# Attention of a diffusion block on TensorE: one query tile of both heads per step, scores two steps ahead, and half of the modulation slabs loaded into the place of the split weights

## The reference, cut to what matters

```
mod  = silu(c) @ w_mod[layer] + b_mod[layer]        # 6 vectors of 1024, for latents and for context
h    = modulate(rms_norm(x, norm1_g), sh1, sc1)
px   = h @ w_in[layer]                              # q, k, v of branches A and B, u of C, gates
y_a  = softmax(q_a k_a' / 8) v_a                    # 8 heads, 512 keys for latents, 256 for context
y_b  = softmax(q_b k_b' / 8 + bias) v_b             # 4 heads, the bias on latent keys only
y_c  = pool_mixer(u)
m    = sum of sigmoid(gate) * (y @ w_branch)        # then w_out and a gated residual
x    = x + g2 * ffn(modulate(rms_norm(x), sh2, sc2))    # dense in layer 0, 8 experts in layer 1
```

## Time and profile before

| | us |
|---|---|
| median of 3 runs (2268.6 to 2272.04) | 2270.48 |
| the profiled execution | 2268.39 |
| its span, first to last instruction | 2266.5 |
| TensorE busy | 2140.1 (94%) |
| attention of layer 0, first scores to the end of the last transpose | 142.55 to 258.85 |
| attention of layer 1, the same | 991.01 to 1072.20 |

### The profile page before, as it was taken

One profiled execution on the slowest core, in us unless ns is written; L12 is line 12 of the kernel. 1 busy time (PEld: TensorE's weight loads), 2 busy tenths in 40 slices (PEclk: granted clock), 3 DMA queues, 4 the chain that ended last, 5 costly groups with the idle time before them and its releaser, 6 DMA issues.

```text
span 2266.5 us, 27521 instructions
## 1 busy us (share of the span) xinstructions
PE 2140.1 (94%) x10750; PEld 1589.7 (70%) x10751; DVE 1147.7 (51%) x1353; ACT 1051.7 (46%) x1139; POOL 1272.5 (56%) x466
## 2 busy tenths in 40 slices
PE   5988899998999998887998999999999999999997
PEld 3874577647788787864997777776767777776775
DVE  2146311231010103345324887878778787878776
ACT  4223322014212123323324766766666666766665
POOL 2300233114545443400421989988988989988996
PEclk8999999998999999898997999999999999999999
DMA  7325521222222222225445999989999999989993
GB/s 296 111 94 223 207 93 75 75 74 103 102 80 106 77 91 93 92 104 205 162 162 204 371 337 353 358 334 352 346 341 345 347 340 351 357 333 352 346 346 142
DMA packets 69640, 503.16 MB, mean 222 GB/s; under 512 B 7744, under 2 KB 7872, under 8 KB 9088
## 3 DMA queue, kind: packets, MB, share of 16 engines
q1 hardware_dynamic: 68976, 497.92, 58.8%
q0 software_dynamic: 528, 3.41, 0.4%
HBM read 500.24 MB, written 1.05 MB: 221 GB/s over the span
## 4 chain that ended last, share of the span: by engine, by line
PE 49%; POOL 32%; issue 12%; DVE 3%; DMA 2%; ACT 1%; SPq 0%; POOLq 0%; DVEq 0%; ACTq 0%
POOL moe_lo L482 31%; PE bank L756 12%; PE bank L758 11%; PE bank L757 11%; PE bank L771 7%; PE bank L784 2%; PE turned L955 2%; PE pv_bank L974 1%; DMA start_slab<-in_w_mod 1%; PE bank L934 1%; DVE s_mx L1859 1%; DMA slab<-in_w_in 1%; POOL w_lo L446 1%; ACT H_NEW L1359 0%; PE bank L939 0%
## 5 line engine op out<-in xcount | busy, mean ns | idle before, releaser
L482 POOL TENSOR_TENSOR moe_lo<-moe_slab,moe_hi 128x512 fp32r<-128x512 f32 x336 | 916.0, 2750 | 163.1 <-ACT moe_hi L1543 161.8
L482 DVE TENSOR_TENSOR moe_lo<-moe_slab,moe_hi 128x1536 fp32r<-128x1536 f32 x336 | 688.3, 2053 | 175.0 <-ACT moe_hi L1543 172.6
L446 POOL TENSOR_TENSOR w_lo<-slab,w_hi 128x2048 fp32r<-128x2048 f32 (+3 forms) x72 | 293.1, 4072 | 741.8 <-ACT w_hi L1316 741.7
L1543 ACT ACTIVATE moe_hi<-moe_slab 128x2048 fp32r<-128x2048 f32 x336 | 629.5, 1906 | 0.1
L756 PE MATMUL bank<-moe_hi,HE_HI 128*96 128x512 f32 x896 | 360.3, 402 | 1.3 <-POOL moe_lo L482 1.2
L758 PE MATMUL bank<-moe_hi,HE_LO 128*96 128x512 f32 x896 | 353.1, 394 | 0.0
L757 PE MATMUL bank<-moe_lo,HE_HI 128*96 128x512 f32 x896 | 351.7, 392 | 0.0
L756 PE MATMUL bank<-H_HI,w_hi 128*128 128x512 f32 (+1 forms) x880 | 325.6, 370 | 17.9 <-POOL H_LO L660 12.7
L757 PE MATMUL bank<-H_LO,w_hi 128*128 128x512 f32 (+1 forms) x880 | 321.9, 366 | 0.0
L758 PE MATMUL bank<-H_HI,w_lo 128*128 128x512 f32 (+1 forms) x880 | 321.8, 366 | 0.0
L1316 ACT ACTIVATE w_hi<-slab 128x2048 fp32r<-128x2048 f32 (+1 forms) x72 | 135.6, 1883 | 166.6 <-PE bank L758 147.8
(11 more groups left out here) (199 smaller groups left out, 2481.9 us busy)
## 6 DMA issues: line engine op xcount, KB each, us to landing
moe_slab<-in_moe_up SPq DMA_DIRECT2D x224, 1024.0 KB, 4.8
moe_slab<-in_moe_w SPq DMA_DIRECT2D x112, 1024.0 KB, 4.8
slab<-in_w_mod SPq DMA_DIRECT2D x40, 1024.0 KB, 4.8
slab<-in_w_in SPq DMA_DIRECT2D x38, 1024.0 KB, 4.8
slab<-in_ffn_w SPq DMA_DIRECT2D x30, 1024.0 KB, 4.8
start_slab<-in_w_mod SPq DMA_DIRECT2D x8, 1024.0 KB, 18.0
slab<-in_w_proj SPq DMA_DIRECT2D x8, 1024.0 KB, 6.9
slab<-in_w_out SPq DMA_DIRECT2D x8, 1024.0 KB, 4.9
```

What stands on the lines that cost most here:

```text
L446: engine.tensor_tensor(lo, raw, hi.bitcast(F32), ALU.subtract).then_inc(done, 1)
L482: engine.tensor_tensor(moe_lo[n][:, blocks, :], moe_slab[k % MOE_RING][:, blocks, :], moe_hi[n][:, blocks, :].bitcast(F32), ALU.subtract). ...
L1543: af(moe_hi[k % MOE_SPLIT][:], moe_slab[k % MOE_RING][:], ACT.Copy).then_inc(moe_hi_ready, 1)
```

## The change

A step is now one query tile of both heads of a latent pair, or both query tiles of both heads of a context pair: 18 steps in layer 0, 12 in layer 1. Scores are made two steps ahead. In each step TensorE makes the scores of step n + 2, one piece of modulation, the transposes of step n, and, where the step before ended a pair, the values of that pair. Bank `turned[g]` holds head g, and ScalarE copies both banks; VectorE copies none. The table is replaced by a rule: of three steps, two have a `mod` and the third a `turned_mod`. The `mod` of every step with n % 3 == 1 (`OUT_OF_RING`) no longer goes through the ring: its two slabs are loaded to `side_slab`, four buffers that lie where `w_hi` and `w_lo` lie. SyncE loads them between the ring's loads, the first two pairs when the last split matmul of the projection (`u`, 1) is done, the others when the `mod` two before in the same place is done. Before the first `high_part` after the attention ScalarE waits for these `mod`s.

The core of the diff:

```diff
+def attention_steps(layer):
+    return [(p, t) for p, (_, _, stream) in enumerate(attention_pairs(layer))
+            for t in range(2 if stream == LAT else 1)]
-MOD_IN_ATTENTION = (
-    [((p + 2) // 2 if p and p % 2 == 0 else None, None, 4 + p) for p in range(12)],
-    [(None, None, 16), (None, 17, 18), (8, None, 19), (9, 20, 21), (10, None, 22), (None, None, 23)])
+MOD_FIRST = (4, 16)
+def mod_beside(layer, s):
+    return None if s % 3 == 2 else MOD_FIRST[layer] + 2 * (s // 3) + s % 3
+def turned_beside(layer, s):
+    return MOD_FIRST[layer] // 2 + s // 3 if s % 3 == 2 else None
...
+        side_slab = [at(f"side_slab{i}", 24 + 8 * i, [P, DC, 256]) for i in range(4)]
...
+            def side_load(i):
+                n = OUT_OF_RING.index(i)
+                layer = int(i >= MOD_FIRST[1])
+                if i < MOD_FIRST[layer] + 4:
+                    wait_full(sp, ("in", layer, ("u", 1)))
+                else:
+                    wait_full(sp, ("mod", OUT_OF_RING[n - 2]))
+                for m in range(2):
+                    sp.dma_start(side_slab[2 * (n % 2) + m][:].rearrange("p k n -> p (k n)"), a["w_mod"][2 * i + m])\
+                        .then_inc(side_in[n % 2], 16)
...
+                if order[n][0] == "mod" and order[n][1] % 2 == 0:
+                    i = order[n][1] // 2
+                    first = MOD_FIRST[i >= MOD_FIRST[1]]
+                    if i == first + 2:
+                        side_load(i - 1)
+                        side_load(i + 1)
+                    elif i > first + 2 and i + 1 in OUT_OF_RING:
+                        side_load(i + 1)
...
 # TensorE
+                def turn(n):
+                    stream = pairs[steps[n][0]][2]
+                    for g in range(2):
+                        pe.wait_ge(p_ready[layer], 2 * n + g + 1)
+                        if n:
+                            pe.wait_ge(turned_out[layer], 2 * n + g - 1)
+                        for t in range(4):
+                            if stream == LAT:
+                                src = P * t
+                            else:
+                                kt, qt = divmod(t, 2)
+                                src = S * qt + P * kt
+                            ins = nc.tensor.transpose(turned[g][:, P * t:P * t + P], PR[:, n % 2, g, src:src + P], ident)
+                        ins.then_inc(turned_full[layer], 1)
...
+                scores(0)
+                scores(1)
+                for n in range(len(steps)):
+                    if n + 2 < len(steps):
+                        scores(n + 2)
+                    if mod_beside(layer, n) is not None:
+                        mod(mod_beside(layer, n))
+                    else:
+                        turned_mod(turned_beside(layer, n))
+                    turn(n)
+                    if n and last_step(layer, n - 1) is not None:
+                        values(last_step(layer, n - 1), n - 1)
+                values(len(pairs) - 1, len(steps) - 1)
...
 # ScalarE
                 exps(0)
+                for n in range(len(steps)):
+                    if n + 1 < len(steps):
+                        exps(n + 1)
+                    if ended(n - 2) is not None:
+                        result(ended(n - 2))
+                    turned_copy(n)
+                if ended(len(steps) - 2) is not None:
+                    result(ended(len(steps) - 2))
+                for i in OUT_OF_RING:
+                    if (i >= MOD_FIRST[1]) == layer:
+                        wait_full(act, ("mod", i))
                 for _ in range(2):
                     high_part()
                 result(len(pairs) - 1)
...
 # VectorE
                 maxima(0)
                 maxima(1)
+                for n in range(len(steps)):
+                    normalise(n)
+                    if n + 2 < len(steps):
+                        maxima(n + 2)
+                    if mod_beside(layer, n) is not None:
+                        mod(mod_beside(layer, n))
+                    else:
+                        turned_mod(turned_beside(layer, n))
```

More of the change, by code:

```diff
@@ L117, in mod @@
     def mod(i):
-        if i not in MOD_AT_START:
+        if i not in MOD_AT_START and i not in OUT_OF_RING:
             slabs.extend([("mod", 2 * i), ("mod", 2 * i + 1)])
@@ L150, in schedule, with scores @@
         fills.extend(("in", layer, ("u", m)) for m in range(layer, 2))
[L151 to L168, removed]
+        steps = len(attention_steps(layer))
+        def scores(n):
+            if n < steps:
+                fills.extend(("score", layer, n, g) for g in range(2))
+        scores(0)
+        scores(1)
+        for n in range(steps):
+            scores(n + 2)
[3 more added lines that the diff above has]
+                turned_mod(turned_beside(layer, n))
         fills.extend(("pool", layer, p) for p in range(2))
@@ L1436, in turned_out @@
[L1436 to L1444, removed]
+                pairs, steps = attention_pairs(layer), attention_steps(layer)
@@ L1840, in attention, with columns @@
             def attention(layer):
[L1841 to L1846, removed]
+                pairs, steps = attention_pairs(layer), attention_steps(layer)
+                def columns(n):
+                    p, t = steps[n]
+                    return (4 * p + 2 * t, 4 * p + 2 * t + 2) if pairs[p][2] == LAT else (4 * p, 4 * p + 4)
@@ L1847, in maxima @@
+                def maxima(n):
+                    p, t = steps[n]
+                    branch, j, stream = pairs[p]
+                    lo, hi = columns(n)
+                    for g in range(2):
+                        key = ("score", layer, n, g)
+                        wait_full(dve, key)
                         if stream == LAT:
-                            key = ("score", layer, u, t)
-                            wait_full(dve, key)
-                            src = acc(key)[:]
                             if branch == "B":
@@ L1886, in attention @@
                 maxima(0)
                 maxima(1)
-                for p in range(pairs):
-                    normalise(2 * p)
-                    normalise(2 * p + 1)
-                    turned_out(2 * p)
-                    group, before, behind = MOD_IN_ATTENTION[layer][p]
-                    if group is not None:
-                        turned_mod(group)
-                    if before is not None:
-                        mod(before)
-                    if p + 1 < pairs:
-                        maxima(2 * p + 2)
-                    mod(behind)
-                    turned_out(2 * p + 1)
-                    if p + 1 < pairs:
-                        maxima(2 * p + 3)
```

154 lines of the change are left out of this document (73 added, 81 removed).

## The result

The changed kernel takes 2207.2 us (median of 4 runs, 2206.6 to 2208.2), the kernel before 2269.5 us beside it. The ratio is 0.9727, with a 95% interval of 0.9711 to 0.9742. The profiled execution took 2208.2 us, its span is 2206.4 us. 2218 was forecast, with a range of 2208 to 2232: the direction and the mechanism were right, and the kernel was 10.6 us faster than the forecast and 0.8 us faster than the lower end of the range.

What follows compares the result with a forecast made beforehand. No engine was full; TensorE's ring waits and lost clock bound both attention stages. Layer 0 29.8 us less, layer 1 22.2, with -0.4 and +1.1: 52.7 us off 2268.4, plus 2.1 for the median, 2218 us; range 2208 to 2232.

Steps and rivals of the forecast that it cites:

- The work: TensorE's work in the attention up to the last transposes: 80.0 us in layer 0, 53.1 us in layer 1.
- Divided rows: TensorE's wait before transposes, 9.5 us in layer 0 of the old kernel, goes except at the start.
- late slabs: TensorE's waits in front of `mod` in layer 1, 6.9 us, go.
- The wait for a bank: TensorE waits 0.5 us for exponentials in steps without values: 3.2 us in layer 0, 3.0 us in layer 1.
- The start: First scores of each layer's attention wait until a bank is freed: 1.9 us in each layer stays.
- The clock: TensorE's lost clock in the attention: 1.4 and 1.0 us kept for the starts, the rest of the loss goes.
- the clock keeps falling: Rival: 0.5 us waits bring TensorE's lower clock back, 22.5 us lost instead of 2.4; 2238 us, 8 in 100.
- the later first gate: Behind layer 0's attention, the first gate starts 8.9 us after the last transposes instead of 8.5: 0.4 us lost.
- The reference point: Gain taken from the profiled execution of 2268.4 us, then 2.1 us added because the old kernel's median is higher.
- the case without waits: Rival: TensorE's work alone in both attention stages with the two starts, 2209 us, 2206 if starts shrink; 9 in 100.
- Behind the last transposes: After the attention: 0.4 us lost in layer 0, 1.1 us gained in layer 1 as the second gate slab loads earlier.

Runs made afterwards that it cites:

- ring_only: Changed kernel without the side buffers, all modulation slabs through the ring of three: 2238.4 us, ratio to the kernel before 0.9873.
- mod_first: Changed kernel with the piece of modulation ahead of the scores in each step, on TensorE and VectorE: 2202.2 us.
- dve_copy: Changed kernel, but VectorE copies the transposed bank of head 1 and ScalarE only that of head 0: 2203.6 us.
- copy_twice: Changed kernel with each of ScalarE's copies of a transposed bank made twice, one after the other: 2240.6 us.
- before: The kernel without the change, in its first profile: profiled execution 2268.4 us, median 2269.5 us.
- before_again: The kernel before the change, unchanged, profiled and timed again: 2262.5 us, median of 10 runs.
- side_only: Kernel before the change with the side buffers added, the order of its attention kept: 2261.7 us, ratio 0.9974.
- one_ahead: Changed kernel with scores made one step ahead instead of two: 2218.3 us.
- after: The changed kernel in its first profile: profiled execution 2208.2 us, median 2207.2 us.
- again2: The changed kernel, unchanged, run once more as a comparison on the same chip: 2208.5 us.

## Why the prediction was right in direction and short in size

**The work: right.** "Work up to the last transposes becomes 80.0 and 53.1 us": busy were 79.85 and 53.15.

**Divided rows and late slabs: right.** Both waits are gone, at the start too. `ring_only` shows that the slabs' part was a condition of the gain and not only the 6.9 us of layer 1 that the trace of before had: without side buffers 25 us of slab waits come back.

**The wait for a bank: right in place, too large in size.** Priced at 3.2 and 3.0 us, measured 2.3 and 1.8: a wait was 0.35 us and not 0.5, and layer 1 had five and not six. `mod_first`, which takes another bank, and `dve_copy`, which frees it earlier, both remove it.

**The start: right**, 1.7 us for 1.9 in each layer.

**The clock: the step that failed.** "I keep 1.4 and 1.0 us of lost clock for the starts." Nothing was lost: the granted clock is 1.00 in both stages. The 1.4 us are what before lost behind its first two waits in layer 0, 1.88 and then 0.63 us. For the 1.0 us of layer 1 no row stood, and the trace of before speaks against it. The same two waits were followed there by pieces at full clock:

```profile
994.88 1.13 PE L934 MATMUL bank<-QK 64*128 64x512 f32 x4 [1.88 <-ACT PR L1431]
996.64 1.09 PE L955 MATMUL turned<-CONST,PR 128*128 128x128 f32 x8 [0.64 <-DVE PR L1873]
```

In the changed kernel the second of the two waits is gone, and the first, 1.69 us, was followed by full clock in both layers, in three profiles. Layer 0 was forecast at 86.5 us and took 83.9, layer 1 at 59.0 and took 56.7; of these 4.9 us the clock is 2.4, the banks 2.1, the starts 0.4.

`copy_twice` shows that a term for the clock was in the right place: with ten waits of 0.8 to 1.9 us in layer 0, in place of six of at most 0.6, the lower level comes back, and the busy time grows by nearly as much as the waits. The rival "the clock keeps falling" is thus a mechanism that this kernel can have. The Trainium skill's page "TensorE: Matmul & The Clock Gate" (A second HAM failure mode) tells of it for short idles with a change of bank; `copy_twice` agrees (clock 0.90), the changed kernel with its waits of mostly 0.35 us does not (1.00). That these waits are too short was argued in the prediction and is what the runs show. At what length it begins they do not show, since waits of 1.61 us and of 1.93 us were followed by the lower level at one place and not at another.

**The stretch between: a term that was missing.** The forecast had +0.4 us for the later first gate, and that came true (8.8 us behind the last transposes, before 8.5). But the whole stretch was 2.9 us shorter. From the first gate to the first scores of layer 1 the program is the same in all kernels, and there the busy time of TensorE differs from profile to profile while its idle time hardly does. "Clock" is the granted clock in the 60 us that begin 480 us behind the first gate:

| first gate to first scores of layer 1 | TensorE busy, us | idle, us | clock |
|---|---|---|---|
| `before` (old order) | 693.8 | 29.9 | 0.94 |
| `before_again` (old order) | 692.6 | 29.9 | 0.94 |
| `side_only` (old order) | 691.2 | 29.9 | 0.97 |
| `one_ahead` (new order) | 693.6 | 30.2 | 0.94 |
| `after` (new order) | 690.2 | 30.2 | 1.00 |
| `again2` (new order) | 689.6 | 30.3 | 0.97 |
| `dve_copy` (new order) | 687.9 | 29.9 | 1.00 |

So the 2.9 us are not a shorter wait. They are clock, and the busy time differs by 5.6 us among profiles of the new order alone. Whether the order ahead of the stretch moves it by a microsecond or two isn't settled: the old order had 691.2 to 693.8 in three profiles, the new one 687.9 to 693.6 in ten.

**The whole miss.** Of the 10.6 us, 4.9 are the two stages and 3.3 the stretch between; the first scores came 0.9 us later, which goes the other way. The last 3.1 us are between the profiled execution and the median: the prediction added 2.1 us, since the median of before lay above its profiled execution, and that of the changed kernel lay 1.0 below its own. No one of these terms is the whole. The range was missed by 0.8 us: with the 2.4 us of clock lost as forecast, or with the stretch as long as forecast, the time would lie inside it.

**The reference point.** The sum was made against an execution of before that had lost 12.3 us to the clock in layer 0. Another one lost 7, and the medians of before were 2265.8, 2266.4, 2265.4 and 2262.5 us later on. The gain is thus 55 to 62 us, according to which executions of before it is held against, while the changed kernel repeats within 3 us. The range's lower end was the case without waits with the clock at 1.00 counted from 2270.5; I had that case at 2206 to 2209 us and then drew the range at 2208. With the two stages as measured and all else as forecast the time would be 2213 us. That it fell under the case without waits, with 4.1 us of waits for a bank still there, is due to the stretch and the reference and not to the change.

**Behind the last transposes: right.** In layer 0 the first gate starts 8.8 us behind them (8.9 forecast); in layer 1 it starts 6.0 us behind them instead of 7.1, which is the 1.1 us of the forecast.

**What stays open.** The lookahead, the copies on ScalarE and the side buffers were each undone by itself. The smaller step and the new places of the modulation were not: they came together in every run, and how much of the 27 us each of them brings isn't shown.

## What to carry to other kernels

Where an engine is busy 80% of a stage and nothing is full, split its busy time too: count the work at full clock from prices and see what is waits, what is clock. Waits can cost up to nearly their own length again in clock (12 us brought 10 in layer 0 of `copy_twice`, 25 us brought 9 in `ring_only`), and removing them gives both back.

A denser order needs its data sooner: steps and side buffers gave 27 and 4 us alone and 59 together. And two edits that each shorten the same chain (`mod_first`, `dve_copy`) need not add up; here the better single one, 2202.2 us, beats the changed kernel and both together.

## What was not expected of the hardware

The clock lost by one unchanged program differs between executions: 93.3 and 88.4 us busy for the same instructions with the same 23.0 us of waits, and of two equal waits in one trace one can be followed by the lower level and the other not. The changed kernel, which has no such waits, has no such spread in that stage: 83.87, 83.87 and 83.89 us in three profiles.
